# Moving the first loads of two stages ahead of the stage, in a three-stage encoder layer on one core

## The reference

```python
h = rmsnorm(x, norm_g);  proj = h @ w_in              # 1024 -> 3584
q, k, v, g_attn, u, g_four = split(proj)              # 12 heads of 64; Fourier part 4 x 64
q, k = rmsnorm(q, q_g), rmsnorm(k, k_g)
for window, dil in ((128, 1), (512, 4), (2048, 16)):  # banded, dilated, T5 bias
    o, lse = dilated_window_attention(q, k, v, rel_bias, window, dil)
attn = sum(softmax(lse over patterns) * o) * silu(g_attn)
four = (Re fft2(u) over positions and channels) @ w_four * silu(g_four)
y = x + concat(attn, four) @ w_out
```

## Time and profile before

| what | us |
|---|---|
| median of three runs | 3899.77 |
| the profiled execution: its own time | 3901.64 |
| its span, first to last instruction | 3899.9 |
| PE busy | 3731.8 (96%) |
| DVE, ACT, POOL busy | 2516.6, 1702.4, 400.3 |
| granted TensorE clock, mean over the span | 0.983 |

### The profile page before, as it was taken

How to read it: one execution, slowest core, us unless ns; L and a number is a source line. 1 busy time by engine, 2 the same in 40 slices (tenths; PEclk the granted TensorE clock), 3 DMA queues, 4 the chain that set the end, 5 groups by cost and what they waited for, 6 DMA issues and landing times. The chain is left out here.

```text
span 3899.9 us, 99819 instructions
## 1 busy us (share of the span) xinstructions
PE 3731.8 (96%) x38254; PEld 3210.4 (82%) x38254; DVE 2516.6 (65%) x7654; ACT 1702.4 (44%) x4499; POOL 400.3 (10%) x674
## 2 busy tenths in 40 slices
PE   6999999999979999999999689999999997999999
PEld 5888888888867777778888579999899997788887
DVE  5666666666646344434444378888898887777775
ACT  3333333333322111111111179898898997333332
POOL 0000000000000000000000133424233341000000
PEclk9999999999999999999999899999999998999999
DMA  4445555544447875777554587787867775666665
GB/s 139 164 158 155 160 166 152 152 162 164 148 147 222 240 213 167 194 196 204 144 147 143 155 235 199 190 214 174 213 172 205 193 194 159 229 240 240 240 241 181
DMA packets 607705, 722.43 MB, mean 185 GB/s; under 512 B 38299, under 2 KB 474651, under 8 KB 604732
## 3 DMA queue, kind: packets, MB, share of 16 engines
q1 hardware_dynamic: 607356, 717.55, 62.1%
HBM read 383.67 MB, written 337.94 MB: 185 GB/s over the span
## 5 line engine op out<-in xcount | busy, mean ns | idle before, releaser
L555 PE MATMUL p_ps<-p_w_hi,p_h_hi 128*128 128x512 f32 (+1 forms) x3072 | 1151.7, 375 | 22.5 <-DVE p_w_lo L873 21.0
L555 PE MATMUL p_ps<-p_w_lo,p_h_hi 128*128 128x512 f32 (+1 forms) x3072 | 1123.5, 366 | 0.0
L555 PE MATMUL p_ps<-p_w_hi,p_h_lo 128*128 128x512 f32 (+1 forms) x3072 | 1122.2, 365 | 0.0
L1258 ACT ACTIVATE att_p<-att_p,att_o 128x256 f32<-128x256 f32 (+2 forms) x1728 | 684.2, 467 | 117.4 <-DVE att_o L1316 116.5
L555 PEld LDWEIGHTS p_ps<-p_w_hi,p_h_hi 128*128 128x128 f32 x3072 | 581.7, 189 | 129.3 <-issue 31.3
L555 PEld LDWEIGHTS p_ps<-p_w_hi,p_h_lo 128*128 128x128 f32 x3072 | 581.3, 189 | 98.5
L555 PEld LDWEIGHTS p_ps<-p_w_lo,p_h_hi 128*128 128x128 f32 x3072 | 582.3, 190 | 92.6 <-issue 1.9
L1316 DVE CUSTOM_DVE_ANT_0 att_p<-att_ps_s,att_bias 128x256 f32<-128x256 f32 (+2 forms) x1728 | 560.4, 381 | 56.4 <-PE att_ps_s L1196 51.1
L1229 PE MATMUL att_ps_o<-att_v,att_p_low 128*64 128x65 f32 x6528 | 437.3, 225 | 9.9 <-issue 9.5
L1229 PE MATMUL att_ps_o<-att_v,att_p_high 128*64 128x65 f32 x6528 | 437.6, 225 | 7.8 <-issue 7.8
L1229 PEld LDWEIGHTS att_ps_o<-att_v,att_p_low 128*64 128x64 f32 x6528 | 403.2, 139 | 26.2 <-issue 11.0
(11 more groups left out here) (108 smaller groups left out, 5159.1 us busy)
## 6 DMA issues: line engine op xcount, KB each, us to landing
scratch_qk<-p_staging SPq DMA_DIRECT2D x72, 1024.0 KB, 5.6
out_o<-scratch_o SPq DMA_DIRECT2D x144, 396.0 KB, 5.4
att_qk_a<-scratch_qk SPq DMA_DIRECT2D x192, 256.0 KB, 4.5
scratch_o<-att_o SPq DMA_DIRECT2D x168, 264.0 KB, 3.4
p_x<-x SPq DMA_DIRECT2D x48, 512.0 KB, 7.0
scratch_h_t<-p_h_hi SPq DMA_DIRECT2D x48, 512.0 KB, 7.5
scratch_h_t<-p_h_lo SPq DMA_DIRECT2D x48, 512.0 KB, 6.5
p_h_hi<-scratch_h_t SPq DMA_DIRECT2D x48, 512.0 KB, 4.4
```

The lines of the kernel that those rows point to most:

```text
L555: ins = pe.matmul(ps[c][:, 0:width[c]], a[s][:, k, :], b[:, k, cols], start=(k == 0 and n == 0), stop=(k == KC - 1 and n == 2))
L1258: ins = act.activation(at, at, ACT.Exp, bias=o[n % BUFS][:, (2 * q + i) % STRETCH, PW + e:PW + e + 1], scale=-1.0)
```

## The change

Three things, each a move of transfers in SP's program:

1. `setup` asks first for x of tile 0 and for `norm_g`, then for its tables, then for the first six weight parts and x of tile 1. The buffers belong to `build` now, so that they exist before `project(0)`.
2. `project(1)` asks for one piece of `qk_b` at the end of each of tiles 31 to 46. `qk_b` lies where `dft_in` and `dft_out` were, which are done by then. The copy of `w_out` is asked for at the end of tile 2.
3. `attention` opens with bias 0, then the values of stretch 0 with four pieces of a behind each quarter of them; rounds 0 to 7 of pair 0 ask for two pieces of a, as in the other pairs.

No arithmetic is changed. The diff, cut to its core (passing the buffers, semaphores and tables through is left out):

```diff
 def setup: @block.sync
+            sp.dma_start(core.x[0][:], io["x"][lane_rows(0), :]).then_inc(core.x_in[0], 16)
+            with nc.allow_non_contiguous_dma(reason="a gain per channel, 4 KiB in all"):
+                sp.dma_start(core.gain[:], io["norm_g"].rearrange("(k p) -> p k", p=P)).then_inc(core.gain_in, 16)
             sp.dma_start(core.ident[:], io["c_ident"]).then_inc(loaded, 16)
...
+            for i in range(STAGES):
+                to, have = weight_load(core, 0, i, core.staging[:, i * n:(i + 1) * n].rearrange("p (k n) -> p k n", n=BANK))
+                sp.dma_start(to, have).then_inc(core.w_in[i], 16)
+                if i == 0:
+                    sp.dma_start(core.x[1][:], io["x"][lane_rows(1), :]).then_inc(core.x_in[1], 16)

 def project: @block.sync, loads
-            for n, (c, ks) in enumerate(units):
+            for n in range(STAGES if half == 0 else 0, len(units)):
                 if n >= STAGES:
                     sp.wait_ge(w_lo_done, n - STAGES + 1)
 def project: step, after the Fourier piece of tile t, m = t - 2
+                    i = m - len(pieces) - 1
+                    if i == 0:
+                        for n in range(2):
+                            sp.wait_ge(piece_out[n], 16 * len(range(n, len(pieces), 2)))
+                    if 0 <= i < B_PIECES:
+                        to, have = region_piece(core, "b", core.qk_b, 0, i)
+                        sp.dma_start(to, have).then_inc(core.b_in, 16)
+                    if m == 0:
+                        sp.dma_start(dram["w_out"], io["w_out"]).then_inc(core.w_out_kept, 16)

+def region_piece(core, name, region, pair, i):
+    base = BASES["ab".index(name)]
+    lanes, part = i // 4, i % 4
+    at = slice(lanes * BANK, (lanes + 1) * BANK)
+    return (region[:, part, at].bitcast(F32),
+            core.dram["qk"][:, bass.ds(pair * 2 + (part // 2 * 2 * PAIRS + part % 2), 1),
+                            base + at.start:base + at.stop].rearrange("p a t -> p (a t)"))

 def attention: @block.sync
                     if g < 8:
-                        each_round = 4 if opening else 2
-                        for i in range(g * each_round, (g + 1) * each_round):
-                            load_piece_of("a", it, i + A_PIECES - 8 * each_round)
+                        for i in range(2):
+                            load_piece_of("a", it, A_PIECES // 2 + 2 * g + i)
...
-            for i in range(B_PIECES):
-                load_piece_of("b", 0, i)
             load_bias(0, 0)
             for n in range(2):
                 for k in range(4):
                     load_values(n, 0, k)
+                    if n == 0:
+                        for i in range(4):
+                            load_piece_of("a", 0, 4 * k + i)
                 load_bias(n + 1, 0)
-            sp.dma_start(dram["w_out"], io["w_out"]).then_inc(w_out_kept, 16)
-            sp.wait_ge(w_out_kept, 16)
             pairs(sp, body)
```

More of the change, by code:

```diff
@@ L56 @@
 PIECE_FIRST = 2
+STAGES, PARTS = 6, 4
 def t5_bucket(rel):
@@ L125, in build @@
             core.line = core.sb(tables, "line", [NH, len(DILS) * LINE])
+            core.x = [core.sb(tables, f"x{i}", [P, D]) for i in range(2)]
+            core.gain = core.sb(tables, "gain", [P, KC])
+            core.staging = core.sb(tables, "staging", [P, STAGES * KC // PARTS * BANK])
+            core.x_in, core.gain_in = [core.sem(f"x_in{i}") for i in range(2)], core.sem("gain_in")
+            core.w_in = [core.sem(f"w_in{i}") for i in range(STAGES)]
             setup(core)
             project(core, 0)
+        with ExitStack() as buffers:
+            core.dft_in, core.dft_out = ([core.sb(buffers, f"dft_{n}{i}", [P, PIECE]) for i in range(2)] for n in ("in", "out"))
+        core.qk_b = core.sb(core.keep, "qk_b", [P, 4, SEQS[1]], F32R)
+        core.b_in, core.w_out_kept = core.sem("b_in"), core.sem("w_out_kept")
         project(core, 1)
-        core.qk_b = core.sb(core.keep, "qk_b", [P, 4, SEQS[1]], F32R)
         core.w_out_in = core.sem("w_out_in")
@@ L207, in _, with weight_units, weight_load @@
                 dve.tensor_copy(core.chan_w[:, gp, :], ps_chan[gp][:, 0:2 * P])
+CHUNKS = (3, 0, 1, 2)
+WIDTH = [BANK, BANK, BANK, HALF - 3 * BANK]
+def weight_units():
+    n = KC // PARTS
+    return [(c, slice(k, k + n)) for c in CHUNKS for k in range(0, KC, n)]
+def weight_load(core, half, n, stage):
+    c, ks = weight_units()[n]
+    source = [half * 2 * DA + c * BANK for c in range(3)] + [4 * DA + half * DF]
+    rows = core.io["w_in"].rearrange("(k p) n -> p k n", p=P)
+    return stage[:, :, 0:WIDTH[c]], rows[:, ks, source[c]:source[c] + WIDTH[c]]
 class Piece:
@@ L257, in project @@
     S = lambda n: core.sem(name(n))
-    STAGES, PARTS = 6, 4
-    w_in, w_hi_done, w_lo_done = [S(f"w_in{i}") for i in range(STAGES)], S("w_hi_done"), S("w_lo_done")
+    w_in = core.w_in if half == 0 else [S(f"w_in{i}") for i in range(STAGES)]
+    w_hi_done, w_lo_done = S("w_hi_done"), S("w_lo_done")
     mm_done = [S(f"mm_done{c}") for c in range(4)]
@@ L281, in project @@
     banks_t = 2
[L282 to L286, removed]
+    order, width, in_part = CHUNKS, WIDTH, KC // PARTS
+    units = weight_units()
     first = lambda t: isinstance(t, int) and t == 0
@@ L321, in project @@
         if half == 0:
-            gain = sb("gain", [P, KC])
-            x = [sb(f"x{i}", [P, D]) for i in range(2)]
+            gain, x = core.gain, core.x
             h = [sb(f"h{i}", [P, D]) for i in range(2)]
@@ L343, in project @@
             dft_fine = [sb(f"dft_fine{i}", [P, PIECE // DF * N2]) for i in range(2)]
-            dft_in, dft_out = ([sb(f"dft_{n}{i}", [P, PIECE]) for i in range(2)] for n in ("in", "out"))
+            dft_in, dft_out = core.dft_in, core.dft_out
         ps = [core.ps(st, name(f"ps{c}")) for c in range(4)]
@@ L389, in _ @@
             if half == 0:
[L390 to L395, removed]
                 for to, g in ((gain_q, "q_norm_g"), (gain_k, "k_norm_g")):
@@ L398, in _ @@
                         sp.dma_start(to[e * HD:(e + 1) * HD, :], io[g].rearrange("(p a) -> p a", a=1)).then_inc(gains_in, 16)
[L399 to L400 removed]
+            else:
+                load_h(0, 0)
+            for n in range(STAGES if half == 0 else 0, len(units)):
                 if n >= STAGES:
                     sp.wait_ge(w_lo_done, n - STAGES + 1)
[L403 to L404 removed]
+                to, have = weight_load(core, half, n, stage[n % STAGES])
+                sp.dma_start(to, have).then_inc(w_in[n % STAGES], 16)
                 if n == 0:
[L406 removed]
+                    load_h(1, 1)
             if half == 1:
@@ L1068, in load_piece_of @@
             def load_piece_of(name, pair, i):
[L1070 to L1075, removed]
+                to, have = region_piece(core, name, region[name], pair, i)
+                sp.dma_start(to, have).then_inc(a_in if name == "a" else b_in, 16)
             def load_w_out(k):
```

9 lines of the change are left out of this document (5 added, 4 removed).

## The result

The changed kernel takes 3868.59 us (median of 4 runs, 3866.53 to 3869.16), the kernel before beside it 3898.14 (4 runs, 3893.42 to 3902.12). The ratio is 0.9924, 95% interval 0.9907 to 0.9941: 29.6 us less, where 24.0 were forecast. The profiled run took 3869.16, its span is 3867.4.

What follows compares the result with a forecast made beforehand. PE was taken as the bound, so only its standing times could be won: -3.0 - 9.7 + 0.5 + 0.7 - 13.0 + 0.5 = -24.0 from 3901.64, said as 3877 us, range 3869 to 3890.

Steps and rivals of the forecast that it cites:

- Start, -3.0: Kernel start: with x asked for ahead of the tables, ACT's first norm starts at 15.8 instead of 18.77, 3.0 us less.
- Rival D: Start: tables wait behind x and the gain, so nothing is gained, 3880.6; chance 0.64 together with the forecast.
- b's pieces, -9.7: Attention's entry: b already loaded during the second projection, so POOL packs from 2225.7 rather than 2235.37, 9.7 us less.
- Twelve pieces of a ahead of the values, +0.5: Attention's opening: stretch 0's last values land about 2237.2, just in time for PE's first weighing; +0.5 us (0 to +6).
- Round 0 and step 24, -13: Pair 0 of attention: from SP's round 0 to POOL's step 24 it runs like pair 1, 13 us less.
- the two terms around it: Pair 0: +0.5 us for values behind pieces of a, +0.7 for later copy-out of the results of steps 0 and 1.
- The 32 pieces are spread over the whole time from the entry: Pair 0: reason given for expecting PE's "issue" waits to end, beyond the pessimistic 5.3 us, within the -13.
- Two signs of the prediction: Pair 0: POOL packs step 24 some 40 us behind SP's round 0, and PE waits 2 to 3 us there.
- Rival A: Pair 0: the a side gives nothing, so the sum is -11.0 and the time 3890.6; chance 0.10.
- The comparison with pairs 1 to 5: Pair 0: modelled on later pairs, 14.4 us less by pair 1's step 24 or 12.2 by whole pairs 1 to 4.
- The copy in tile 2, +0.5: Second projection: the w_out copy stands right ahead of h for tile 5, which might land late; +0.5 us (0 to +5.4).
- ring order: Second projection: DMA engines serve one queue in order, so h cannot pass the copy; 5.4 us wait when engines are backed up.

Runs made afterwards that it cites:

- experiment 6: Changed kernel with all of stretch 0's values asked for ahead of the 16 pieces of a: first copy-out 14.4 us after the first score, total 3873.29 us.
- experiment 5: Changed kernel without the pieces of a asked for ahead: pair 1's first packing at 168.8 us; with the w_out copy back at the entry, 171.4 (waited for) and 173.0.
- experiment 2: First projection's h moved: 96 bytes in the changed kernel, 0.9963 of the kernel before; in the kernel before, 96 bytes 0.9997, 32 bytes 22.83 us a tile.
- experiment 4: Changed kernel with the w_out copy asked for in tile 30 of the second projection instead of tile 2: tile 5 takes 22.7 us, total 3869.37 us.
- the nine kernels of the table: Before, changed, buffer places alone, and kernels with the first projection's h, or h and combine's m, moved by padding: first projection 22.56 to 22.93 us a tile.

## Why the prediction was wrong

- **Start, -3.0: right.** -2.75, in the way described; the tables are late by 1.07 us, not 0.9. Rival D did not happen.
- **b's pieces, -9.7: right.** The entry's wait fell by 9.6, POOL runs from clearing to packing without a stop, and bias 0 was not late.
- **Twelve pieces of a ahead of the values, +0.5: too small.** The first copy-out is 1.9 to 4.7 us late in four traces, within the bound of 6. The step took 0.92 us for each transfer, and that was too little for the values behind a's pieces: with the values ahead of them the first copy-out is on time again (experiment 6).
- **Round 0 and step 24, -13: wrong in cause, and too large.** With the two terms around it pair 0 was to gain 11.8; it gained 7.1. "The 32 pieces are spread over the whole time from the entry" is the step that failed. As it was built, with the values behind a's pieces, the spread is worth nothing: without it pair 0 is as short (experiment 5). Of the gain 2.6 to 4.2 us are the copy of `w_out`, which no longer runs beside a's pieces, by one trace each; where the rest comes from is open. Two signs of the prediction came true all the same (POOL packs step 24 42.3 us behind round 0, and PE waits 2.2 there), so they could not tell the causes apart. Part of the excess is one trace: the step 24 that the prediction read, 70.1 us behind the first score, is the latest of seven kernels with the same attention, whose mean is 68.0. Rival A was right about the a side, but missed that a gain comes from other edits. The comparison with pairs 1 to 5 was the wrong model: those have no copy and no opening either, and I read all of the difference as the effect of their order.
- **The copy in tile 2, +0.5: mis-sized, by another route.** The prediction asked when h would land and gave what stands behind it "a tile more". But SP is one program: when its stores cannot be issued, all behind them is late, the Fourier piece by 6 us. The cost, 5.5, is the wait of 3.55 and the clock behind it. That it is near the upper bound is luck, since that was made for another reason. As to ring order, which the Trainium skill ("DMA: Bandwidth & Descriptors", section "Queues, rings and completion order") made the case to expect, the traces agree: h, issued 4.2 us behind the copy, took 17.2 us and landed at 1257.3, 2 us behind the copy, and in experiment 4 the h behind the copy landed 1.1 us behind it. The 5.5 us are close to the 5.4 by that rule, but no wait for h is among them.
- **Missing: the first projection, -15.3.** This is the step that took the time out of the range: the sum had this stage at nothing, without a reason. The diff says that buffers belong to `build` now, and the trace of before has the same 128x512 matmul 233 ns apart in one projection and 227 in the other; the prediction looked at neither. Without it the change gives 12 to 14 us (experiment 2), some 3884 to 3887 against the 3898.14 beside it: inside the range, but 7 to 10 us above the forecast.

## What to carry to other kernels

Where one instruction runs at two rates in two stages of a trace, find out why before tuning anything else; here two paddings, of 224 and 448 bytes, were worth more than the change without its luck (27.6 us in one run against 11.6). A change that moves an allocation moves the place of everything behind it, and so can alter stages it does not touch: compare the rate of the unchanged work too. The long copy cost time here where the issuing engine was held and a load that PE needed stood behind, so for each place that a copy could stand in, look at what that engine issues in the next 20 us, not only at the load right behind it.

## What the runs showed of the hardware

- 128x512 float32 matmuls of w (moving) and h (stationary) started 227 ns apart (median) when the distance between the two tiles in SBUF was a multiple of 256 bytes, and 232 to 234 when its remainder was 32, 64, 96 or 128: in the nine kernels of the table, three stages. Those of 256 columns started 120 apart in the first case and 114 to 119 in the second. Why is open.
- SP's issue of one store of values, 0.6 us as a rule here, took up to 3.11 while the copy was landing and 4.25 at 1271.99, 17 us after it had landed. That the queue was full then is my reading; the trace shows the issues alone.
- A wait of PE cost more than its length: 3.55 us of standing in tile 5 were followed by 3.4 us at a granted clock of 0.5, and the tile was 5.5 us longer.
- The five pairs that no edit touched took between 875 and 889 us in 16 traces, so a single run cannot show a gain of 5 us behind them.
